# FFN ends of a two-layer decoder trunk: a down product moved between the halves of a gate/up panel, a square ahead of the last silu, a low part cut in two

## The reference

```python
modulate = lambda t, i: rms_norm(t, norm_g[l, i]) * (1.0 + scale(i)) + shift(i)
h = modulate(x, 0)
x = x + 0.5 * gate(0) * swiglu(h, ffn_wg[l, 0], ffn_wu[l, 0], ffn_wd[l, 0])
h = modulate(x, 1)
...
x = x + gate(1) * (y @ w_out[l])
h = modulate(x, 2)
x = x + 0.5 * gate(2) * swiglu(h, ffn_wg[l, 1], ffn_wu[l, 1], ffn_wd[l, 1])

def swiglu(h, wg, wu, wd):
    return (jax.nn.silu(h @ wg) * (h @ wu)) @ wd
```

## Time and profile before

| what | value |
|---|---|
| median of three runs | 1281.35 us (1281.32 to 1281.73) |
| the profiled execution: its own time | 1281.08 us |
| its span, first to last instruction | 1279.3 us |
| PE busy | 1234.3 us (96% of the span) |
| DVE busy | 965.5 us (75%) |
| ACT busy | 546.9 us (43%) |
| DMA | 293.44 MB, mean 229 GB/s |
| granted TensorE clock | 0.995 of full speed |

### The profile page before, as it was taken

The page is one execution under the profiler, slowest core; times in us unless marked ns, Lnnn a source line. Parts: engine busy times, 40 slices in busy tenths (PEclk is TensorE's granted clock), DMA queues, the critical chain, the costliest instruction groups (busy, mean ns, idle before and its releaser), DMA issues.

```text
span 1279.3 us, 13844 instructions
## 1 busy us (share of the span) xinstructions
PE 1234.3 (96%) x5440; PEld 957.3 (75%) x5448; DVE 965.5 (75%) x1341; ACT 546.9 (43%) x576; POOL 2.2 (0%) x5
## 2 busy tenths in 40 slices
PE   3999999999999999999999999999999999999997
PEld 2588887766776887888878888876676678888885
DVE  5698886699997576988668888668999866644443
ACT  3343434532344555344355433354323564634431
POOL 0000000000000000000000000000000000000000
PEclk9999999999999999999999999999999999999999
DMA  9989994444233539889747889545532335455540
GB/s 375 416 317 373 375 377 177 184 179 166 100 113 118 191 111 377 345 342 356 301 170 276 343 344 356 193 162 204 188 133 99 132 132 196 167 197 189 193 177 34
DMA packets 52913, 293.44 MB, mean 229 GB/s; under 512 B 6640, under 2 KB 6896, under 8 KB 27120
## 3 DMA queue, kind: packets, MB, share of 16 engines
q1 hardware_dynamic: 51120, 289.38, 60.4%
q10 hardware_dynamic: 1728, 3.17, 0.7%
HBM read 291.45 MB, written 1.07 MB: 229 GB/s over the span
## 4 chain that ended last, share of the span: by engine, by line
PE 90%; DVE 3%; DMA 3%; ACT 2%; issue 1%; SPq 0%; DVEq 0%
PE ps L329 24%; PE ps L331 24%; PE ps L330 24%; PE ps L348 12%; DMA raw<-in_weights 2%; PE ps L515 1%; PE ps L396 1%; PE ps L537 1%; DMA ada_raw<-in_ada_w 1%; DVE hF L1084 1%; PE ps L526 0%; PE ps L485 0%; ACT L715 0%; DVE w_lo L997 0%; PE ps L380 0%
## 5 line engine op out<-in xcount | busy, mean ns | idle before, releaser
L997 DVE TENSOR_TENSOR w_lo<-raw,w_hi 128x2048 fp32r<-128x2048 f32 x176 | 401.0, 2286 | 40.8 <-ACT w_hi L709 40.5
L709 ACT CAST w_hi<-raw 128x2048 fp32r<-128x2048 f32 x176 | 334.5, 1910 | 163.7 <-PE ps L331 82.9
L329 PE MATMUL ps<-w_hi,hA_hi 128*128 128x512 f32 (+1 forms) x992 | 397.7, 401 | 2.9 <-DVE hA_lo L997 2.9
L331 PE MATMUL ps<-w_hi,hA_lo 128*128 128x512 f32 (+1 forms) x992 | 385.2, 388 | 0.0
L330 PE MATMUL ps<-w_lo,hA_hi 128*128 128x512 f32 (+1 forms) x992 | 384.6, 388 | 0.0
L329 PEld LDWEIGHTS ps<-w_hi,hA_hi 128*128 128x128 f32 x992 | 187.4, 189 | 46.6 <-issue 11.9
L330 PEld LDWEIGHTS ps<-w_lo,hA_hi 128*128 128x128 f32 x992 | 187.7, 189 | 38.5 <-issue 3.3
L331 PEld LDWEIGHTS ps<-w_hi,hA_lo 128*128 128x128 f32 x992 | 187.2, 189 | 38.9
L1186 DVE SCALAR_TENSOR_TENSOR work<-conv_in,par,work 128x256 f32<-128x256 f32 x480 | 193.7, 478 | 0.0
L1012 DVE SCALAR_TENSOR_TENSOR product<-ada_raw,c_bc 128x1024 f32<-128x1024 f32 x144 | 171.6, 1220 | 15.6 <-DMA ada_raw<-in_ada_w 15.2
L348 PE MATMUL ps<-raw,hF 128*128 128x512 f32 x384 | 171.6, 598 | 5.5 <-ACT hF L734 5.5
(11 more groups left out here) (120 smaller groups left out, 741.8 us busy)
## 6 DMA issues: line engine op xcount, KB each, us to landing
raw<-in_weights SPq DMA_DIRECT2D x200, 1024.0 KB, 4.8
ada_raw<-in_ada_w SPq DMA_DIRECT2D x144, 512.0 KB, 6.7
gate_bc<-gate_scratch ACTq DMA_DIRECT2D x6, 512.0 KB, 6.3
x<-in_x_tok SPq DMA_DIRECT2D x1, 1024.0 KB, 7.4
out_tok<-xn_h SPq DMA_DIRECT2D x4, 256.0 KB, 2.2
c_bc<-in_c_row SPq DMA_DIRECT2D x1, 512.0 KB, 4.4
c_bc<-in_g_row SPq DMA_DIRECT2D x1, 512.0 KB, 5.6
mask_all<-in_mask SPq DMA_DIRECT2D x1, 416.0 KB, 16.3
```

The lines of the kernel that those rows point to most:

```text
L329: nc.tensor.matmul(out_ap, stat[0], mov[0], start=start, stop=False)
L331: return nc.tensor.matmul(out_ap, stat[1], mov[0], start=False, stop=stop)
L709: nc.scalar.copy(w_hi[:, s % HI, :], raw[:, p % RAW, :]).then_inc(hi_done, 1)
L997: return nc.vector.tensor_tensor(dst, whole, hi_part.bitcast(F32), ALU.subtract)
```

## The change: what it does

At the end of every FFN, PE's `pa` product for tile 1 is cut after two of its four chunks, and the down product of block 10 for tile 0 runs between the cut parts; `panel_done` for `pa` is signalled by the second part. On ACT, `norm_square` moves ahead of `silu` of tile 1, and `norm_std` moves ahead of `mid_high(1)`. On DVE, `lo(end + 1)` becomes two instructions over half of the columns each (`lo_half`), one ahead of `hidden(1)` and one behind it, and `norm_scale` moves ahead of `mid_low(1)`; the end of the last FFN keeps its order on DVE. At the end of the mixing sub-layer the first half of `lo(end + 1)` goes ahead of `norm_scale`, the second behind it.

```diff
--- before.py
+++ after.py
@@ -339,10 +339,10 @@
                 else:
                     pe.wait_ge(lo_done, splits(p) + 1)
 
-            def k_half(p, h, tt, b, out_ap, last=None):
+            def k_half(p, h, tt, b, out_ap, last=None, chunks=range(4)):
 
                 t = slice(tt * P, (tt + 1) * P)
-                for i in range(4):
+                for i in chunks:
                     k, c = 4 * b + i, slice(512 * i, 512 * i + 512)
                     if is_whole(p):
                         mm = nc.tensor.matmul(out_ap, hF[:, k, t], raw[:, p % RAW, c], start=(k == 0), stop=(k == KC - 1))
@@ -350,7 +350,8 @@
                         hi, lo = parts(p)
                         mm = three(out_ap, (h[0][:, k, t], h[1][:, k, t]), (hi[:, c], lo[:, c]), k == 0, k == KC - 1)
                 if tt == 1:
-                    mm.then_inc(panel_done, 1)
+                    if chunks[-1] == 3:
+                        mm.then_inc(panel_done, 1)
                 elif last is not None:
                     mm.then_inc(last, 1)
 
@@ -449,8 +450,9 @@
                 k_half(pb, hA, 0, 1, ps[:, gu(j), :], half_done)
                 down(f, j - 1, 0)
                 turn(f, j, (0,))
-                k_half(pa, hA, 1, 0, ps[:, gu(j) + 1, :])
+                k_half(pa, hA, 1, 0, ps[:, gu(j) + 1, :], chunks=range(2))
                 down(f, j, 0, last=first_done)
+                k_half(pa, hA, 1, 0, ps[:, gu(j) + 1, :], chunks=range(2, 4))
                 k_half(pb, hA, 1, 1, ps[:, gu(j) + 1, :])
                 down(f, j - 1, 1, (0,))
                 turn(f, j, (1,))
@@ -824,11 +826,11 @@
                 silu(f, j, (0,))
                 mid_high(f, j, 0)
                 hi(end + 1)
+                norm_square(n + 1, 0)
                 silu(f, j, (1,))
-                norm_square(n + 1, 0)
                 preload(ACT.Sqrt)
+                norm_std(n + 1, 0)
                 mid_high(f, j, 1)
-                norm_std(n + 1, 0)
                 if n + 1 < NORMS - 1:
                     norm_full(n + 1, 0)
                     norm_hi(n + 1, 0, 0)
@@ -1003,6 +1005,14 @@
                 dve.wait_ge(hi_done, s + 1)
                 minus(w_lo[:, p % RAW, :], raw[:, p % RAW, :], w_hi[:, s % HI, :]).then_inc(lo_done, 1)
 
+            def lo_half(p, half):
+                s = splits(p)
+                dve.wait_ge(hi_done, s + 1)
+                c = slice(half * (PW // 2), (half + 1) * (PW // 2))
+                op = minus(w_lo[:, p % RAW, c], raw[:, p % RAW, c], w_hi[:, s % HI, c])
+                if half:
+                    op.then_inc(lo_done, 1)
+
             def ada(q):
                 g, w, k = ADA[q]
                 dve.wait_ge(ada_in[q % ADA_RING], 16 * (q // ADA_RING + 1))
@@ -1155,12 +1165,15 @@
                 lo(end)
                 mid_low(f, j, 0)
                 x_update(n, 0)
+                if n + 1 == NORMS - 1:
+                    hidden(f, j, (1,))
+                    mid_low(f, j, 1)
+                    return
+                lo_half(end + 1, 0)
                 hidden(f, j, (1,))
+                lo_half(end + 1, 1)
+                norm_scale(n + 1, 0)
                 mid_low(f, j, 1)
-                if n + 1 == NORMS - 1:
-                    return
-                norm_scale(n + 1, 0)
-                lo(end + 1)
                 norm_full(n + 1, 0)
                 norm_lo(n + 1, 0, 0)
                 norm_lo(n + 1, 0, 1)
```

## The result

The changed kernel takes 1271.05 us, the median of six runs (1269.48 to 1274.04); the kernel before took 1280.92 us in six (1279.91 to 1281.73). The ratio is 0.9926, with a 95% interval from 0.9911 to 0.9942: 0.74% faster. The direction is as forecast, 6.9 us were forecast to be won and about 9.5 were (0.74% of 1281; the two medians differ by 9.9). The profiled execution of the changed kernel took 1272.22 us with a span of 1270.4; for the kernel before it was 1281.08 and 1279.3.

A forecast was written before the change was run, and what follows sets the result against it. PE's waits at the FFN and mixing ends, 7.8 us in all, were taken as the stock to win. 3 x 1.8 + 0.75 + 0.75 = 6.9 us off 1281.08 gave 1274.2 us, range 1272.6 to 1277.2.

The forecast's parts named there:

- the lower end of the range: Whole kernel: removing every PE wait gives 7.8 us, with nine restarts of about 0.08 at most 8.5: 1272.6 us.
- An FFN end: Three FFN ends with a sub-layer behind: next sub-layer starts at 220.1 instead of 221.87, 1.8 us won each, bounds 1.2 to 2.08.
- The last end: Last FFN end: square ends before silu, so end_lo comes 0.75 us earlier; 0.75 won, bounds 0.4 and 0.8.
- a mixing end: Two mixing ends: the low part's first half fits DVE's gap before the reciprocal; 0.37 us won, twice.
- The cut: PE at FFN ends: moved down starts at 206.00 without a stall for mid_lo; x update done 1.36 us earlier, at 211.48.
- The late high part of end + 1: ACT at the first FFN end: pa ends 2.72 us later, so hi(end + 1) starts at 210.34, ends at 212.25.
- The halves: DVE at FFN ends: 1.2 us each; the second ends at 215.45, the root at 215.5, cover nearly used up.
- A: FFN ends: ACT's queue pushes the root back, so it comes no earlier; 4.1 us won, 1277.0 us; chance 0.10.
- B: Mixing: the gain before it is lost again at the convolution wait; 3.3 us won, 1277.8 us; chance 0.06.
- C: ACT: a drain after each table load puts the root off by 1.38 us; 1.4 won, 1279.7 us; chance 0.04.
- D: Next sub-layer: panel end + 2, asked for 2.72 us later, comes too late; slower, 1286 us; chance 0.02.
- E: PE's starts don't change, because another wait of the same length stands behind each removed one; 1281 us; chance 0.02.

The follow-up runs named there:

- no_cut: Changed kernel with PE's cut undone: the whole of pa for tile 1 ahead of the down of block 10, tile 0; 1274.89 us, ratio to before 0.9955.
- late: Changed kernel with one whole low part, lo(base + 27), moved ahead of the last convolution steps on DVE; 1278.16 us, ratio to before 0.9982.
- fill: Changed kernel with PE multiplying tile 0 of the last gate's first panel ahead of the last convolution transposes, where it waited for DVE; 1265.83 us, ratio to before 0.9887.
- fill_tail: As fill, and the low part of panel base + 28 goes behind DVE's four low parts of the layer-norm output; 1265.16 us, ratio to before 0.9881.
- again_b: The changed kernel once more, without an edit, for another trace; that execution took 1273.69 us.
- again_c: The changed kernel once more, without an edit, for another trace; that execution took 1273.08 us.
- before_third: The kernel before once more, without an edit, for another trace; that execution took 1281.13 us.

## Why the prediction was wrong

**The step that failed** is the lower end of the range: "what is not there, PE spends on work that the change leaves alone", and from it "8.5 is the most that can be won: 1272.6". It took PE's busy time as fixed. As a bound on what the order wins, 8.5 held: the order won 8.1. As a bound on the time of a run it failed. In the first trace before, the matmuls at half clock behind the two convolution waits cost 3.3 us (2 x 1.64), and how much of that an execution of the changed kernel has varies: 0, 1, 2 and 2 falls in four traces. The sum had no term for it; the earlier trace rows showed the wait that carries it, and the prediction set that wait aside as "no target".

**How far below the range the result lies is in part luck.** The six runs have a median of 1271.05 us, all thirteen 1272.2. Only one of the six has a trace (1272.22, one fall), so that the three near 1269.6 had no fall is not shown. The base was high as well: the sum starts from an execution of 1281.08 us with two falls, where 39 runs of the kernel before have a median of 1280.5.

**Three terms were sized too small**, with the mechanism right. An FFN end brought 2.04 and not 1.8: all but 0.04 of its two waits. By 0.2 us the root came earlier: in the trace ACT starts an instruction before the one ahead has ended (the square 1.81 after the start of a cast of 1.91, silu 0.09 after the start of an accumulator read of 0.19), and the sum took them end to end; by 0.15 `norm_turn` came earlier, the part that the sum named and left out (216.15 to 217.20 is 1.05, not 1.21). The next product then came 3.79 behind `norm_turn` and not 3.7, which takes 0.1 back. The last end brought 0.85 (0.75) and a mixing end 0.46 (0.37): the sum had counted PE's restart behind a wait, 0.08 each, only in the upper bound, which fits the size of these differences. That makes 7.9 instead of 6.9, and 8.1 by the executions with falls and start taken out; the other 0.2 is not assigned. By the order alone the time would have been 1281.1 - 8.1 = 1273.0, inside the range.

**Point by point.** The cut: no wait for mid_lo, as said; and it is needed, 0.75 per end (`no_cut`). The late high part of end + 1: as said, to 0.01 us, and no wait of PE came of it. ACT: `hidden(1)` ended at 215.18 and PE turned at 215.33, with no wait, where 0.2 was set down. The halves: 1.22 us each, 1.2 forecast; the second ended at 216.32, 0.1 before the root's end at 216.43, so the thin cover held. end_lo: no wait.

**The rivals.** A fell: the root came 1.1 us earlier against the turn of tile 0 (10.59 after it, 11.70 before). B fell: the waits for the convolution are 5.0 us, 5.1 before, and the 8.1 us are kept. C fell: the load from 214.74 to 216.02 is followed at 216.04 by the small activation and at 216.15 by the root. The Trainium skill, "ScalarE: Activation LUTs", section "What ACT_TABLE_LOAD costs", agrees with the trace in the load (1283 ns) and not in the drain of about 1380 ns that it adds. D and E fell: PE waits for no panel there, and no other wait stands behind those removed.

**Left open:** why a wait of 2.5 us is followed by a fall of the clock in some executions and not in others, and why the changed kernel's runs spread over 4.7 us where those before spread over 2.5. No run here settles either.

## What to carry to other kernels

Count PE's waits one by one for the stock that an order can win, but look at the granted clock behind each wait as well: a wait can cost again in the work that follows it. An edit that moves an instruction forward is worth what the instructions behind it then allow: here the halves were worth 1.13 us per FFN end with the other two parts in place and 0.76 without them. When a part of one engine's queue is too long to fit one gap, cut it so that each piece fits a gap that is already there.

## What the runs showed of the hardware

TensorE's clock fell to its lower level behind 14 of the 22 PE waits of 2.52 us in eleven traces, and behind both waits of 4.7 us in the one trace of `late`; with PE fed it didn't fall in the traces of `fill` and `fill_tail`. Behind PE's waits of 1.6 us or less (for xn_h, mid_lo, mid, the low part of h, end_lo) it fell in no trace. A step of a matmul of 512 columns is 0.227 us at the upper level and 0.43 at the lower one (398.65 on in the profile after), and one fall cost 1.64 us. The first transposes of block 0 come between 53.30 and 54.82 us in seven executions of two kernels that are the same up to there: 1.5 us of the spread between runs lie ahead of that. PE is busy for 29.6 to 29.9 of the 30 us from 24 to 54 us in all seven, so what differs there is how fast its first matmuls ran, and not a wait. The granted clock there reads 0.91 to 0.93 in `again_b`, `again_c` and `before_third` and 1.00 in the other four, which differ among themselves by as much (53.30 to 54.82), so that reading alone doesn't explain it.
